# One short self-wait of TensorE in the second unit of every weight segment

## What is computed

```python
h = rmsnorm(x, ln_g);  proj = h @ w_in          # then three branches
x = x + mixed @ w_out                           # first block
h = rms_norm(x, norm_mix_gain);  proj = h @ w_in_2
merged = sigmoid(g_a) * (o_a @ w_branch_a) + sigmoid(g_b) * (o_b @ w_branch_b)
x = x + merged @ w_out_2
q = rms_norm(x, norm_ffn_gain) @ w_query        # picks 16 experts a head
act = gelu(expert_u[ids] . x);  x = x + sum(gates * act * expert_v[ids])
```

## Time and profile before

| | us |
|---|---|
| median of 3 runs | 3048.19 |
| the three runs | 3044.38, 3048.19, 3060.18 |
| the profiled execution | 3022.95 |
| its span, first to last instruction | 3020.9 |
| TensorE busy | 2891.5 |
| GpSimd busy | 2303.2 |
| ScalarE busy | 1319.7 |
| VectorE busy | 1093.1 |

### The profile page before, as it was taken

How to read it: one execution, slowest core, us unless ns; L and a number is a source line. 1 busy time by engine, 2 the same in 40 slices (tenths; PEclk the granted TensorE clock), 3 DMA queues, 4 the chain that set the end, 5 groups by cost and what they waited for, 6 DMA issues and landing times.

```text
span 3020.9 us, 59158 instructions
## 1 busy us (share of the span) xinstructions
PE 2891.5 (96%) x24230; PEld 2840.4 (94%) x24230; DVE 1093.1 (36%) x1550; ACT 1319.7 (44%) x1549; POOL 2303.2 (76%) x925
## 2 busy tenths in 40 slices
PE   7999979999999988999999888999999999999998
PEld 7999979899999986999999888999999999999998
DVE  6003365344000013324399898130404013043422
ACT  5454452554534342344453554344343434434333
POOL 6777640489788860878788646899998989999996
PEclk9999989999999996999999999999999999999999
DMA  6544420255555540446455444656565565656653
GB/s 240 178 156 170 153 84 0 79 174 193 178 181 194 183 153 0 167 167 209 153 179 182 180 183 182 222 181 230 185 224 180 207 224 181 230 187 223 222 195 125
DMA packets 85673, 523.89 MB, mean 173 GB/s; under 512 B 8657, under 2 KB 23121, under 8 KB 24402
## 3 DMA queue, kind: packets, MB, share of 16 engines
q1 hardware_dynamic: 68258, 489.12, 46.1%
q10 hardware_dynamic: 17328, 33.56, 3.0%
HBM read 503.77 MB, written 18.87 MB: 173 GB/s over the span
## 4 chain that ended last, share of the span: by engine, by line
PE 35%; POOL 34%; issue 27%; DVE 2%; ACT 1%; POOLq 1%; DVEq 0%
PE banks L1289 35%; POOL wlo L395 34%; POOLq L394 0%; DVE xlo L787 0%; PE banks L1385 0%; POOLq L389 0%; DVE T L780 0%; DVE dec L967 0%; DVE ycv L923 0%; ACT za L683 0%; DVE gv L940 0%; DVE gv L942 0%; ACT za L673 0%; ACT za L672 0%; ACT za L671 0%
## 5 line engine op out<-in xcount | busy, mean ns | idle before, releaser
L395 POOL TENSOR_TENSOR wlo<-raw,whi 128x1024 fp32r<-128x1024 f32 x920 | 2298.5, 2519 | 665.9 <-ACT whi L418 664.1
L418 ACT ACTIVATE whi<-raw 128x1024 fp32r<-128x1024 f32 x920 | 948.3, 1056 | 746.9 <-PE banks L1289 739.4
L1289 PE MATMUL banks<-xhi,whi 128*128 128x256 f32 x4928 | 676.3, 280 | 16.2 <-ACT xhi L497 6.9
L1289 PE MATMUL banks<-xhi,wlo 128*128 128x256 f32 x4928 | 671.5, 279 | 7.0 <-POOL wlo L395 6.5
L1289 PE MATMUL banks<-xlo,whi 128*128 128x256 f32 x4928 | 671.6, 279 | 1.8 <-DVE xlo L787 1.8
L1289 PEld LDWEIGHTS banks<-xhi,whi 128*128 128x128 f32 x4928 | 617.6, 190 | 19.1 <-issue 11.7
L1289 PEld LDWEIGHTS banks<-xhi,wlo 128*128 128x128 f32 x4928 | 614.7, 189 | 9.8 <-POOL wlo L395 9.8
L1289 PEld LDWEIGHTS banks<-xlo,whi 128*128 128x128 f32 x4928 | 616.2, 189 | 2.4 <-DVE xlo L787 2.4
L848 DVE TENSOR_TENSOR X<-banks,X 128x256 f32 (+1 forms) x112 | 47.5, 424 | 719.7 <-PE banks L1289 719.7
L1289 PE MATMUL banks<-hid_lower,whi 128*128 128x256 f32 x2048 | 274.0, 276 | 0.0
L1289 PEld LDWEIGHTS banks<-hid_lower,whi 128*128 128x128 f32 x2048 | 251.5, 188 | 0.0
(11 more groups left out here) (347 smaller groups left out, 2210.7 us busy)
## 6 DMA issues: line engine op xcount, KB each, us to landing
raw<-in_w_exp SPq DMA_DIRECT2D x256, 1024.0 KB, 4.8
raw<-in_w_in SPq DMA_DIRECT2D x132, 1024.0 KB, 5.0
raw<-in_w_out SPq DMA_DIRECT2D x32, 1024.0 KB, 5.0
raw<-in_w_br SPq DMA_DIRECT2D x16, 1024.0 KB, 5.0
raw<-in_w_q SPq DMA_DIRECT2D x16, 1024.0 KB, 5.0
gates<-gst ACTq DMA_DIRECT2D x16, 1024.0 KB, 4.5
gch<-gates ACTq DMA_DIRECT2D x7, 2048.0 KB, 12.8
raw<-in_w_kv SPq DMA_DIRECT2D x8, 1024.0 KB, 9.7
```

The lines of the kernel that those rows point to most:

```text
L395: pool.tensor_tensor(wlo[:, s, :, :], raw[:, j, h * HALF:(h + 1) * HALF, :], whi[:, s, :, :].bitcast(F32), ALU.subtract).then_inc(lo_ready, 1)
L418: act.activation(whi[:, (2 * j + h) % 4, :, :], raw[:, j, h * HALF:(h + 1) * HALF, :], ACT.Copy).then_inc(hi_ready, 1)
L1289: return nc.tensor.matmul(o, lhsT, rhs, start=start, stop=stop, **k)
```

## The change

Unit 1 of each segment gets one wait of TensorE for itself. In its first half the eighth matmul (the last hi x whi) signals a new semaphore `beat`, and after the first lo x whi matmul TensorE waits for it, so the second lo x whi matmul, the tenth of the unit, starts only after the eighth has ended. `beats` counts the pauses, so that the wait can be on a constant. For this every segment writes out its first pair, and the loop starts at 1. To make room for the semaphore, `ws_ld` and `sk_ld` become one, `tab_ld`.

```diff
+            beats = [0]
+            def pause(k, z):
+                if k == HALF - 1:
+                    z.then_inc(beat, 1)
+                    beats[0] += 1
+                elif k == 0:
+                    pe.wait_ge(beat, beats[0])
-            def unit_body(u, j, hi, lo, par, paired=False, fresh=None, between=None):
+            def unit_body(u, j, hi, lo, par, paired=False, fresh=None, between=None, paused=False):
...
                     for k in range(HALF):
                         upper_x(k)
-                        mm(oo, whi[:, s0 + h, k, :], hi[:, tile(k), :], start=opens and k == 0, stop=False)
+                        z = mm(oo, whi[:, s0 + h, k, :], hi[:, tile(k), :], start=opens and k == 0, stop=False)
+                        if paused and h == 0 and k == HALF - 1:
+                            pause(k, z)
                     def with_lower_x(stop):
                         for k in range(HALF):
                             lower_x(k)
                             z = mm(oo, whi[:, s0 + h, k, :], lo[:, tile(k), :], start=False, stop=stop and k == HALF - 1)
+                            if paused and h == 0 and k == 0:
+                                pause(k, z)
...
             def segment(u0, n, paired=False, hi=xhi, lo=xlo, fresh=None, between=None):
-                first = int(fresh is not None)
-                for j in range(2 * first):
-                    unit_body(u0, j, hi, lo, u0 // 2, paired, fresh if j == 0 or paired else None, between if j == 0 else None)
-                with pe.Fori(first, n // 2) as i:
+                for j in range(2):
+                    unit_body(u0, j, hi, lo, u0 // 2, paired, fresh if j == 0 or paired else None, between if j == 0 else None, j == 1)
+                with pe.Fori(1, n // 2) as i:
                     for j in range(2):
                         unit_body(i * 2 + u0, j, hi, lo, i + u0 // 2, paired)
...
-            sp.dma_start(wst[:], ap["ws"]).then_inc(ws_ld, 16)
-            sp.dma_start(bs_row[:], ap["bs"]).then_inc(ws_ld, 16)
+            sp.dma_start(wst[:], ap["ws"]).then_inc(tab_ld, 16)
+            sp.dma_start(bs_row[:], ap["bs"]).then_inc(tab_ld, 16)
...
-            sp.dma_start(skt[:], ap["sub_keys"]).then_inc(sk_ld, 16)
+            sp.dma_start(skt[:], ap["sub_keys"]).then_inc(tab_ld, 16)
...
-            dve.wait_ge(ws_ld, 32)
+            dve.wait_ge(tab_ld, 32)
...
-            pe.wait_ge(sk_ld, 16)
+            pe.wait_ge(tab_ld, 48)
```

More of the change, by code:

```diff
@@ L290, in program @@
         v_chain, a_chain = sem("v_chain"), sem("a_chain")
-        cst_in, x_ld, ws_ld, sk_ld, out_st = (sem(n) for n in ("cst_in", "x_ld", "ws_ld", "sk_ld", "out_st"))
+        cst_in, x_ld, tab_ld, out_st = (sem(n) for n in ("cst_in", "x_ld", "tab_ld", "out_st"))
         mem_ld = [sem(f"mem_ld{q}") for q in range(4)]
@@ L295, in program @@
         lin_src, lin_hi, lin_lo, lin_lo2 = sem("lin_src"), sem("lin_hi"), sem("lin_lo"), sem("lin_lo2")
-        conv_used = sem("conv_used")
+        conv_used, beat = sem("conv_used"), sem("beat")
         signals = {}
```

## The result

The changed kernel takes **3002.49 us** (median of 4 runs, 2998.27 to 3004.68), the kernel before, on the same chip, 3046.28 us (4 runs, 3035.98 to 3060.18). The ratio is 0.9852 (0.981 to 0.9893): faster by 1.5%. The forecast of 3010 lies 7.5 us above it, and its own range of 2998 to 3028 holds it. All ratios here leave out runs over 1.5% above the fastest of their kernel, so the 1.4% is without two runs of seven, at 3068 and 3074 us; by the means of all runs there it is 0.7%.

A forecast was written before the change was run, and what follows sets the result against it. TensorE was taken as the bound, its matmuls spaced 113.3 or 117.8 ns. From 3022.95 us, less 27 for faster spacing, plus 7.6 for pauses, gave 3003; plus 6.6 for slow landings, 3010, own range 2998 to 3028, overall 2998 to 3063.

The forecast's parts named there:

- TensorE as the bound, and the two rhythms: TensorE, 96% busy, is slowest; its matmul stream holds 113.3 or 117.8 ns spacing until an interruption draws between them.
- The pause (Part 1): Unit 1's tenth matmul waits for the eighth: 0.23 us at each of 33 waits, +7.6 us (3.6 to 9.9).
- The new draw (Part 2): Slow stretches of TensorE's stream restart fast after the pause: 6040 of 6600 matmuls gain 4.5 ns, 27 us.
- The relief, put at nothing: Pauses would be free where GpSimd's `wlo` is later than TensorE; no such saving was counted.
- The written-out pair and the joined counters (Part 3): Peeling each loop's first pair moves the branch, and joining `ws_ld` and `sk_ld` changes no order: nothing.
- The sum: Profiled execution of the kernel before, less the faster spacing, plus the waits: 3022.95 - 27 + 7.6 = 3003 us.
- The share that lands slow: 8% of the 18,300 matmuls behind pauses end at the slow spacing, 4.5 ns each: +6.6 us, giving 3010.
- The 19 gaps: Interruptions of the wide matmul stream at full clock in the profile: 16 left it fast, 3 slow, none of nine shortest.
- The gap no rhythm: The 25 us between profiled execution and median isn't spacing, so it adds: 3035 us (3028 to 3042); chance 0.12.
- No better than chance: The pause in unit 1 draws like any earlier interruption, leaving only its cost: 3056 us (3045 to 3063); chance 0.16.
- The clock: Each of 33 pauses drops TensorE's granted clock to half, 2.6 us apiece: 3096 us; chance 0.03.
- The pause lands slow: TensorE's phase may be alike at all 33 pauses, making all 18,300 matmuls behind them slow: 3086 us; chance 0.15.

The follow-up runs named there:

- the 1.4%: The changed kernel, unaltered, on a third chip beside the kernel before: 3006.38 us against 3049.45, ratio 0.986.
- the first trace: Profiled execution of the changed kernel from its original measurement against the kernel before: 2998.27 us.
- the second: Trace of the changed kernel run again, unaltered, on another chip against the kernel before: median 3017.65 us, ratio 0.9938.
- the third trace: Trace of the changed kernel run unaltered on a third chip against the kernel before, taken from its first run there: 3068.41 us.
- three other traces: Kernel before, unedited (3045.6 us); changed kernel without any pauses (3047.86 us); changed kernel without pauses in the expert segments (3038.53 us).
- the first comparison: Original measurement of the changed kernel against the kernel before on one chip, 4 runs each: 3002.49 against 3046.28 us, 0.9852.
- the second trace of the kernel before: The kernel before, unedited, profiled once more: 3045.6 us.
- chip 2: Chip where the unaltered change took 3017.65 us (0.9938) and the change without expert pauses 3038.53 (0.9993), against the kernel before at 3039.88.
- chip 9: Chip where the change plus a second pause in the unit's other half took 3078.29 us, 1.012 against the kernel before.

## Why the prediction held, point by point

**TensorE as the bound, and the two rhythms.** Right. The time of TensorE is the time of the kernel in all traces here, and every long window of them lies at 113.2 to 113.6 or at 117.4 to 118.1 ns, with pauses and mixtures in it.

**The pause (Part 1).** 0.23 us was forecast, 0.233 measured, 7.7 us for 33. As the records log it, both parts came out, each at the end of its range: the tenth matmul starts 0.334 us after the eighth (0.34 to 0.41 was said), 0.11 us late, and the restart adds the other 0.12 us, since the eleventh starts 0.22 us after it and not 0.11. The wait was that of the row in which TensorE is the waiter: the weight load follows the end of the eighth by 0.06 us. Where the 0.12 us lie within the tenth is less sure: it lasts 0.38 us where others last 0.28, and the next weight load is logged 0.11 us after its start and not right behind it. So it may well wait for its own weights first; then it is the loading that isn't hidden, and not an array run dry, that the 0.12 us are. No run separates the two.

**The new draw (Part 2).** 27 us forecast, 27.1 measured: 881 slow groups became 121. The agreement to 0.1 us is luck. The windows held 6600 slow matmuls, the whole trace 7048; and 560 were to stay slow, where 968 did. The two misses, 448 and 408 matmuls of 4.5 ns, cancel. (The window from 361.7 us gives 122.0 ns by the prediction's own division, and not 117.6 to 118.8, for the other sums in it; its matmuls were slow all the same.)

**The relief, put at nothing.** Nearly right. In the experts the gaps by late `wlo` shrink: at each of five places the eight matmuls up to and with the gap took 146 ns each before and 117 to 121 after, about 0.2 us: 1 us. VectorE's wait for `picks`, which the prediction saw as the way on for TensorE's lead, fell from 9.4 to 3.7 us:

```profile
DVE gs L1200 <- ACT picks L725: 3.7, 1, 3.7
```

**The written-out pair and the joined counters (Part 3).** Little or nothing: the kernel without a pause is 0.3% slower (0.1 to 0.5%), which is at the edge of what these runs can tell.

**The sum.** 3003 us against the profiled execution, measured 2998.27. The 5 us lie outside the terms: 2.2 less at half clock and restarts together, and 3.3 less in small matmuls. No experiment was made on these, and they differ as much between two traces of the kernel before (2.7 and 4.0 us), so they aren't shown to be a gain of the change.

**The share that lands slow.** This is the step that was mis-sized: "half that share, 8%" as an even thinning, 6.6 us. No one share holds. It was 0 of 33 in the first trace, 6 of 33 in the second (22.5 us in slow groups, 18 more than the first), and 27 of 33 in the third trace. The 19 gaps from which it was taken are waits for other engines in one execution. That none of the nine short ones ended slow was luck too: the late `wlo` near 1980 us, with the 0.26 us of five of the nine, ended slow in three other traces. Pauses of one kind within one execution go more alike than independent draws would. In the first comparison the 0 was met, hence 3002 rather than 3010.

**The rivals.** *The gap no rhythm* is out: the second trace of the kernel before has the 25 us as slow groups, and the median fell by more than the profile did (44 against 25 us). *No better than chance* is out as a rule: the same code without pauses gains nothing, with them it gained 1.4 to 1.5% on two chips, and on chip 2 the pauses in the experts alone are worth 21 us; but there a part of them lands slow, and the gain is 0.6%. *The clock* is out: every window shown here that has pauses in it has 1.00. On this the rule that the prediction took from the Trainium skill ("TensorE: Matmul & The Clock Gate", "A second HAM failure mode: psum-queue depth-cycling") isn't borne out at this frequency; the kernel with two pauses in the unit doesn't show it either, with a clock of 1.00 in both of its windows. *The pause lands slow* had 0.15 and didn't come in the median, but it does exist: in 2 of 21 executions of the change, and in all 6 of its sibling with two pauses on chip 9. Its premise, one phase at all 33 places, is nearer to the first and the third trace than the forecast's even share, though not to the second (27 fast, 6 slow); what was wrong in it was that the phase is the same in every execution.

**Still open.** What sets the side, for a pause or for most of an execution. From a fast stream, pauses that end at either spacing differ by 1 to 2 ns in the records (the waiting weight load 332 to 333 ns after the eighth's start against 331 to 332, the matmul after the tenth 222 to 224 ns behind it against 221 to 222), which is a sign and not a cause. Why 117.8 ns exist at all is open too.

## What to carry to other kernels

Divide the windows of the busiest engine by its instructions before believing its busy share: two spacings at the same clock can hide in a 96% that hardly moves, and how long one of them lasts tells what an interruption is worth (here 27.1 us for 7.7). Of several such waits take the one that leaves a fast stream fast, at the least price, and judge it by many executions on several chips. Where the profiled execution and the median differ by nearly a per cent, look at a second trace of the kernel before first.

## What the hardware showed that was not expected

- A stream of wide matmuls at a granted clock of 1.00 runs at 113.3 or at 117.8 ns a matmul and keeps to it, for 8067 matmuls in a row in one window, until something interrupts it.
- The same short wait does three things by where it stands. On the ninth matmul it flipped the spacing (32 of 32, in the one trace there is). On the tenth it ended fast at 33 and at 27 of 33 pauses in two traces of the change and slow at 27 of 33 in the third. On the eleventh it kept all 51 fast streams fast and sped up 9 of 13 slow streams, at 0.12 us in place of 0.23.
- An instruction of TensorE that waits for another of TensorE pays for the way out and back: the signal of the eighth is logged 0.29 us after its start, the waiting weight load 0.04 us later and its matmul 2 ns behind that; the next matmul follows 0.22 us on in place of 0.11.
- One restart can be worth more than all 33 pauses: a `wlo` late by 0.26 us left the stream fast in one trace and slow in three, and on it hung 1113 groups of eight, about 40 us.
- How the pauses end differs from execution to execution of one kernel: on one chip one kernel ran from 3014 to 3079 us, and on another the change took 3068 and 3074 us in two runs beside five at 3002 to 3008.
